# Eighty more columns in a shared SBUF buffer, so that the operands of the attentions' plain float32 products start 64 bytes apart modulo 256

## What is computed

```python
h = rms_norm(x, attn_norm)
q_r, k_r, v_r, g_r, q_m, k_m, v_m = split(h @ w_in)
# retention branch: 4 heads, 128 wide for q and k, 256 wide for v
o_r = retention_chunkwise(rotary(q_r), rotary(k_r) * 128 ** -0.5, v_r)
y_ret = (head_group_norm(o_r) * silu(g_r)) @ w_ret_o
# softmax branch: 8 heads, 128 wide, causal over the 256 tokens
o_m = moba_attention(rms_norm(q_m), rms_norm(k_m), v_m)
y_moba = o_m @ w_moba_o
gate_ret, gate_moba = split(sigmoid(h @ w_gate + b_gate))
x = x + (gate_ret * y_ret + gate_moba * y_moba) @ w_out
h = rms_norm(x, ffn_norm)
u_gate, u_val = split(causal_depthwise_conv(h @ w_up))
x = x + (silu(u_gate) * u_val) @ w_down
```

## Time and profile before

| | us |
|---|---|
| median of three runs | 469.57 |
| the profiled execution, its own time | 469.32 |
| its span, first to last instruction | 467.5 |
| TensorE busy | 460.7 (99% of the span) |
| VectorE busy | 300.1 (64%) |
| ScalarE busy | 256.6 (55%) |
| GpSimd busy | 16.7 (4%) |

### The profile page before, as it was taken

The page is one execution under the profiler, slowest core; times in us unless marked ns, Lnnn a source line. Parts: engine busy times, 40 slices in busy tenths (PEclk is TensorE's granted clock), DMA queues, the critical chain, the costliest instruction groups (busy, mean ns, idle before and its releaser), DMA issues.

```text
span 467.5 us, 7814 instructions
## 1 busy us (share of the span) xinstructions
PE 460.7 (99%) x3121; PEld 424.8 (91%) x3121; DVE 300.1 (64%) x371; ACT 256.6 (55%) x370; POOL 16.7 (4%) x28
## 2 busy tenths in 40 slices
PE   7999999999999999999999999999999999999997
PEld 5799899888888999999999788999999999988886
DVE  4759992764665547345338676688788888884313
ACT  5866443047774839351445355777777766663300
POOL 0100000311110001000000000000000000000000
PEclk9999999999999999999999999999999999999999
DMA  8995564244445534943453733626555555538002
GB/s 279 422 405 189 205 237 182 91 179 155 148 155 207 217 111 131 365 160 144 161 201 131 264 135 130 238 72 237 201 186 196 191 203 195 196 128 322 1 1 90
DMA packets 14698, 87.20 MB, mean 187 GB/s; under 512 B 1616, under 2 KB 2512, under 8 KB 5328
## 3 DMA queue, kind: packets, MB, share of 16 engines
q1 hardware_dynamic: 14256, 85.25, 48.7%
q0 software_dynamic: 416, 1.57, 1.0%
HBM read 85.77 MB, written 1.05 MB: 186 GB/s over the span
## 4 chain that ended last, share of the span: by engine, by line
PE 85%; DVE 7%; DMA 4%; ACT 2%; issue 1%; SPq 1%; ACTq 0%; DVEq 0%
PE bank L393 15%; PE bank L395 15%; PE bank L394 15%; PE bank L347 5%; PE bank L346 5%; PE bank L345 5%; DMA w_raw<-weights_dram 4%; PE bank L645 4%; PE bank L644 4%; PE bank L647 4%; DVE w_pair L942 3%; PE bank L414 2%; PE bank L550 2%; PE bank L551 2%; PE bank L552 2%; ACT w_pair L664 1%
## 5 line engine op out<-in xcount | busy, mean ns | idle before, releaser
L942 DVE TENSOR_TENSOR w_pair<-w_raw,w_pair 128x2048 fp32r<-128x2048 f32 x73 | 165.9, 2288 | 85.5 <-ACT w_pair L664 85.3
L664 ACT ACTIVATE w_pair<-w_raw 128x2048 fp32r<-128x2048 f32 x73 | 138.2, 1919 | 31.0 <-PE bank L647 17.1
L393 PE MATMUL bank<-h_hi,w_pair 128*128 128x256 f32 x512 | 143.8, 281 | 1.0 <-DVE w_pair L942 1.0
L395 PE MATMUL bank<-h_hi,w_pair 128*128 128x256 f32 x512 | 143.1, 279 | 0.0
L394 PE MATMUL bank<-h_lo,w_pair 128*128 128x256 f32 x512 | 143.0, 279 | 0.0
L393 PEld LDWEIGHTS bank<-h_hi,w_pair 128*128 128x128 f32 x512 | 96.4, 188 | 1.3 <-DVE w_pair L942 1.2
L394 PEld LDWEIGHTS bank<-h_lo,w_pair 128*128 128x128 f32 x512 | 96.4, 188 | 0.1
L395 PEld LDWEIGHTS bank<-h_hi,w_pair 128*128 128x128 f32 x512 | 96.4, 188 | 0.0
L393 PE MATMUL bank<-a_hi,w_pair 128*128 128x256 f32 x192 | 54.0, 281 | 0.0
L394 PE MATMUL bank<-a_lo,w_pair 128*128 128x256 f32 x192 | 53.7, 280 | 0.0
L395 PE MATMUL bank<-a_hi,w_pair 128*128 128x256 f32 x192 | 53.6, 279 | 0.0
(11 more groups left out here) (140 smaller groups left out, 569.4 us busy)
## 6 DMA issues: line engine op xcount, KB each, us to landing
w_raw<-weights_dram SPq DMA_DIRECT2D x73, 1024.0 KB, 4.9
w_raw<-weights_dram SPq DMA_DIRECT2D x6, 512.0 KB, 8.8
w_raw<-weights_dram SPq DMA_DIRECT2D x4, 256.0 KB, 4.9
ys<-x_dram SPq DMA_DIRECT2D x2, 512.0 KB, 9.8
xs<-x_dram POOLq DMA_DIRECT2D x1, 1024.0 KB, 8.1
area<-decay_dram SPq DMA_DIRECT2D x1, 768.0 KB, 13.3
out_dram<-ys SPq DMA_DIRECT2D x3, 256.0 KB, 2.0
xs<-x_chan_dram SPq DMA_DIRECT2D x1, 512.0 KB, 6.4
```

The costliest lines, as they stand in the source:

```text
L393: mm(o, s_hi, r_hi[:, k, :], start=(k == 0 and m % 2 == 0), stop=False)
L395: ins = mm(o, s_lo, r_hi[:, k, :], start=False, stop=(k == KT - 1 and m % 2 == 1))
L664: A(w_parts(n, r)[0], raw[r][:, :], ACT.Copy).then_inc(hi_ready, 1)
L942: tt(lo, raw[r][:, :], hi.bitcast(f32), ALU.subtract).then_inc(lo_ready, 1)
```

## The change

`area` grows from 8192 to 8272 columns, and six tiles in it start later: `kr_t` by 16 columns (64 bytes), `v_r` by 80 columns (320 bytes, 64 modulo 256), `km_t` by 48 columns (192 bytes), `g_t` and `v_m` by 80 columns. `xs`, `ys`, `ident`, `mask` and `col`, which lie behind `area`, start 80 columns (320 bytes, 64 modulo 256) later. Nothing ahead of `area` moves, nor do the tiles of `area` that are not named in the diff.

```diff
-        area = sb("area", [P, 8192])
+        area = sb("area", [P, 8272])
...
-        kr_t = area[:, 3072:4096].rearrange("p (h s) -> p h s", h=RET_HEADS)
-        v_r = area[:, 4096:6144].rearrange("p (t d) -> p t d", t=NT)
+        kr_t = area[:, 3088:4112].rearrange("p (h s) -> p h s", h=RET_HEADS)
+        v_r = area[:, 4176:6224].rearrange("p (t d) -> p t d", t=NT)
...
-        km_t = area[:, 4096:6144].rearrange("p (h s) -> p h s", h=MOBA_HEADS)
-        g_t = area[:, 6144:8192].rearrange("p (k s) -> p k s", k=KT)
-        v_m = area[:, 6144:8192].rearrange("p (t d) -> p t d", t=NT)
+        km_t = area[:, 4144:6192].rearrange("p (h s) -> p h s", h=MOBA_HEADS)
+        g_t = area[:, 6224:8272].rearrange("p (k s) -> p k s", k=KT)
+        v_m = area[:, 6224:8272].rearrange("p (t d) -> p t d", t=NT)
```

## The result

The changed kernel took a median of 470.94 us against 469.57 us before; the ratio is 1.0028, with a 95% interval of 1.0015 to 1.004. So it is slower by 1.3 us by that ratio (1.4 us by the two medians), where 0.09 us of gain was forecast, and it lies 0.3 us above the range's upper end of 470.6 us.

The account below looks back on a forecast made before the run. TensorE's own rate was taken to bound the kernel. Twenty heads saving 4.5 ns each give 0.09 us, all other terms zero: 469.57 - 0.09 = 469.48, rounded to 469.5 us, range 468.5 to 470.6 us.

Parts of the forecast that it names:

- What bounds the kernel: Whole kernel: TensorE's own rate sets the time, busy 460.7 of 467.5 us, with 4.1 us of waits.
- The plain products' price: Attention score heads: 654.7 ns a head falls to 650.2 ns at distance 64; 20 heads save 0.09 us.
- the 5.1 ns of the earlier trace: Retention's output products, already 64 bytes apart: 431.8 ns each, 5.1 ns above the columns' time, taken for the moved products.
- All split products: unchanged: Split products: only plain products and uses of moved buffers could be affected, so no cost was counted here.
- the moved transposes: Transposes: they keep distance 0 because ident moves with its partners; cost 0.
- if any split product's price changes: Sign in the profile after that would prove the prediction wrong; the down projection was to keep 1.400 and 1.360 us.
- The row itself: Down projection: six split products take 1.400 us with weights unshifted, 1.360 us shifted by 32 bytes, 2.9% more.
- a bound for 13.1 us of plain products: Score heads: the down projection's 2.9% applied to their 13.1 us would be 0.39 us lost.
- No effect at all: Rival, plain products: no distance matters or the moves are to no purpose; 469.6 us, chance 0.23.
- worse by distance, up to 0.39 us: Rival, plain products: new distance is worse, 470.0 us at most; chance 0.13 shared with loads' loss up to 0.5 us.
- The rival of the loads: Loads of x into xs and ys at the start slow off 256-byte boundaries: 470.0 to 471.0 us; full size chance 0.04.
- the largest loss that I could name: Loads' loss at its full size, at the start: 1.4 us, chance 0.04.

Follow-up runs that it names:

- behind: Kernel before with the buffer 80 columns longer and its tiles unmoved, so only xs, ys, ident, mask and col move by 64 bytes modulo 256; ratio 1.0036.
- h_later: Kernel before with h_hi, h_lo, a_hi and a_lo 32 bytes later, besides them only two small tiles moved; 470.34 us in a single execution.
- h64: Kernel before with activations 32 bytes later and SHIFT doubled to 16: activations-moving products at distance 64, weights-moving ones at 0; 466.82 us, ratio 0.9945.

## Why the prediction was wrong

- **What bounds the kernel** held: TensorE's own rate, no new wait, and each product's price is the kernel's.
- **The plain products' price** was mis-sized. The term was 20 heads x 4.5 ns = 0.09 us, and it measured nothing: the trace's records, to the nanosecond, give 654.7 ns a head before and 654.3 ns after, but 654.3 ns in the second trace of before too. The step that failed here was to take the 5.1 ns of the earlier trace rows as due to its distance. In `behind` those twelve products were 128 bytes apart, and eleven took 82.71 - 77.97 = 4.74 us, 430.9 ns: the same to the resolution of the rows. What is above the columns' time in a head of 256 and 128 columns (434 ns and 221 ns in both kernels, by the records) is not distance, and why it is more than in a row of 256-column products no run shows.
- **"All split products: unchanged", and so at no cost**, is the step that made the sum wrong. Their addresses did not change, their price did: 1.03 us in the long run (117.8 instead of 116.7 ns for each of 912) and 0.1 to 0.2 us in shorter stretches. The prediction costed the moved transposes at zero because their own distance stayed; it had no rival in which one product's place changes the price of those behind it. Its list of what would prove it wrong did name it ("if any split product's price changes").
- **The earlier trace rows was used for the wrong products.** The row itself was read rightly: it is an effect of distance, as `h_later` and `h64` showed. But I used it only as a bound for 13.1 us of plain products, when it told that split products, most of the kernel, have prices that placement sets. From the Trainium skill's page "SBUF — State Buffer", section "Who interferes with whom", by which TensorE's reads wait for nobody, the prediction drew that no distance should matter. That does not describe what is seen: the 512-column split products cost 226.7 ns at 0 bytes and 233.3 ns at 32, and the 256-column ones 113.3 to 120.0 ns by placement. By what mechanism, no run shows.
- **The rivals.** "No effect at all" was right of the plain products and wrong of the kernel; "worse by distance, up to 0.39 us" fell. The rival of the loads fell as well, since the loss lies behind 83 us, and the first product of the queries' block starts within the scatter of the start (83.08 and 83.46 us, and in the repeats a difference of the other sign). One piece of it seems real but small: from the last down half's first product to the end of the span, the traces with `ys` moved are 0.03 to 0.05 us longer than those with it in place (8.27 to 8.28 against 8.23 to 8.24 us, among kernels whose down projection has 1.360 us for six products). In the first two traces the difference lies behind VectorE's last instruction, in the final store: 2.14 against 2.10 us. That fits stores which read from 64 bytes off, though nothing here tests the cause.
- **The range** ended at 470.6 us, since the largest loss that I could name was put down with a chance of 0.04. The measured 0.28% still lies within the 0.3% that was given 0.88, but that is luck: the causes counted there were a gain, no effect and a loss of up to 0.5 us, and none of them is what happened.

## What to carry to other kernels

Where one engine is the bound with back-to-back products, read the spacing of its products stretch by stretch and not only their mean: two or three fixed values for one form are a sign that placement or entry decides, and 1% of the long run here was 1.0 us, more than all that the plain products had above their columns' time (0.29 us). Try the places of the commonest product's operands first, and re-time after any change of the buffers' layout, since it can move the rhythm of products that it does not touch. An edit of that kind is judged by two or more traces of the same stretch, which agreed here to 0.01 us in the long run, better than by times that scatter by 1 us. One trace is not enough: a stretch near the varying start (G_R1) had two rhythms in one program.

## What the runs showed of the hardware

For split products in fp32r at a granted clock of 1.00, ns a product in unbroken stretches:

| form | distance in bytes, moving less stationary | price |
|---|---|---|
| 256 columns, activations moving | 32 | 116.7 or 117.8; 120.0 once |
| the same | 64 | 113.3 or 117.8 |
| the same | 96 | 120.0 |
| the same | 128 | 118.7 |
| 512 columns, weights moving | 0 | 226.7 |
| the same | 32 or 64 the other way | 233.3 |
| the same | 96 the other way | 234.2 |

- For the products with the weights moving, the price went with the distance whichever operand was moved (1.400 us for six at 32 with either one moved, 1.360 us at 0 with neither and with both). For the 256-column products with the activations moving only the activations were ever moved against the weights, so the table can't tell the distance from the place of the activations themselves.
- A rhythm lasts as long as nothing else comes between, for 912 products and 107 us; it can change where transposes or plain products stand between, and one transpose more changed it.
- Over both kernels' two traces each, the choice was the same each time in the long run; but it depends on what moved behind the buffer together, and on a transpose 5.7 us earlier. In G_R1, behind the varying start, it differed between executions of one program: 11.39 and 11.29 us in the changed kernel, and 11.29 and 11.39 us in the two traces of the kernel before with the extra transpose, which comes long after. That the exact moment of entry is what decides would explain all of this; no row resolves it, and it stays open.
- Why the distance matters, and whether 256 bytes is its period, stays open too: the edits kept the other places modulo 256 but for small tiles, and none tested another period. Nothing between 0 and 32 bytes was tried.
